# Bias lines made first and spread straight from SBUF, and one norm moved by a step, in a hybrid attention block

## The reference

```python
u = rmsnorm(h, attn_norm_g)
qa, ka, va, qb, kb, vb = split(u @ w_in)
oa = swa_sink_attention(qa, ka, va, sinks, rel_bias)   # 8 heads, chunks of 64, window of 128 keys, T5 bias
ob = diff_attention(qb, kb, vb, lam, ..., rel_bias)    # 4 heads, two softmaxes each, block-causal, T5 bias,
                                                       # then rmsnorm per head over its 128 columns
h = h + concat(oa, ob) @ w_out
h = h + square(relu(rmsnorm(h) @ w_up)) @ w_down
h = h + sigmoid(rmsnorm(h) @ w_gate) * (p @ w_ple)
y = rmsnorm(h, final_norm_g)
```

## Time and profile before

| | |
|---|---|
| median of 3 runs | 1303.7 us (1301.81 to 1304.3) |
| profiled execution | 1304.3 us, span 1302.5 us |
| TensorE busy (matmuls) | 1281.1 us, 98% of the span |
| VectorE, ScalarE, GpSimd busy | 445.5, 377.4, 478.9 us |
| mean granted TensorE clock | 0.993 of full speed |
| DMA | 82.91 MB, mean 64 GB/s |

### The profile page before, as it was taken

The page is one execution under the profiler, slowest core; times in us unless marked ns, Lnnn a source line. Parts: engine busy times, 40 slices in busy tenths (PEclk is TensorE's granted clock), DMA queues, the critical chain, the costliest instruction groups (busy, mean ns, idle before and its releaser), DMA issues.

```text
span 1302.5 us, 15895 instructions
## 1 busy us (share of the span) xinstructions
PE 1281.1 (98%) x6089; PEld 1026.7 (79%) x6089; DVE 445.5 (34%) x598; ACT 377.4 (29%) x690; POOL 478.9 (37%) x235
## 2 busy tenths in 40 slices
PE   7999999999999999999999999999999999999997
PEld 5777777777677888888888888888888888888886
DVE  5254655557765442211112211122111222223224
ACT  6344444455555422110011100111100112223221
POOL 3220202233335764322233322333222335675743
PEclk7999999999999999999999999999999999999999
DMA  6711101213512221111111111111111111113203
GB/s 225 259 33 33 33 17 33 49 50 97 146 34 78 84 81 38 47 49 46 49 47 50 47 48 48 48 48 48 48 48 48 48 48 49 48 58 92 61 1 130
DMA packets 139296, 82.91 MB, mean 64 GB/s; under 512 B 22185, under 2 KB 134870, under 8 KB 139126
## 3 DMA queue, kind: packets, MB, share of 16 engines
q1 hardware_dynamic: 138870, 81.19, 20.7%
q10 hardware_dynamic: 384, 1.15, 0.2%
HBM read 73.91 MB, written 10.77 MB: 65 GB/s over the span
## 4 chain that ended last, share of the span: by engine, by line
PE 94%; DVE 3%; ACT 1%; DMA 1%; issue 1%; SPq 0%; DVEq 0%; ACTq 0%
PE ps L994 61%; PE ps L1018 22%; PE ps L1127 3%; PE ps L1150 3%; PE ps L1138 1%; PE ps L1214 1%; PE ps L1200 1%; PE ps L1187 1%; DMA x_raw<-in_x 1%; ACT e_a L790 1%; PE ps L1060 1%; PE ps L1076 0%; PE ps L1031 0%; PE ps L1320 0%; DVE kmax L1559 0%
## 5 line engine op out<-in xcount | busy, mean ns | idle before, releaser
L527 POOL TENSOR_TENSOR w_lo<-w_raw,w_hi 128x1024 fp32r<-128x1024 f32 x110 | 268.7, 2443 | 723.9 <-ACT w_hi L698 453.6
L698 ACT CAST w_hi<-w_raw 128x1024 fp32r<-128x1024 f32 x70 | 73.9, 1055 | 452.3 <-PE ps L994 452.3
L994 PE MATMUL ps<-z_hi,w_hi 128*128 128x512 f32 x624 | 193.4, 391 | 0.0
L994 PE MATMUL ps<-z_lo,w_hi 128*128 128x512 f32 x624 | 192.2, 389 | 0.0
L994 PE MATMUL ps<-z_hi,w_lo 128*128 128x512 f32 x624 | 192.1, 389 | 0.0
L1018 PE MATMUL ps<-u_hi,w_hi 128*128 128x512 f32 x416 | 177.2, 426 | 1.7 <-DVE o_bt L1501 1.7
L1018 PE MATMUL ps<-u_hi,w_lo 128*128 128x512 f32 x416 | 164.3, 395 | 0.0
L1018 PE MATMUL ps<-u_lo,w_hi 128*128 128x512 f32 x416 | 163.8, 394 | 0.0
L994 PE MATMUL ps<-u_lo,w_hi 128*128 128x512 f32 x512 | 157.6, 389 | 0.0
L994 PE MATMUL ps<-u_hi,w_hi 128*128 128x512 f32 x512 | 157.6, 389 | 0.0
L994 PE MATMUL ps<-u_hi,w_lo 128*128 128x512 f32 x512 | 157.6, 389 | 0.0
(11 more groups left out here) (163 smaller groups left out, 1343.7 us busy)
## 6 DMA issues: line engine op xcount, KB each, us to landing
w_raw<-in_w_up SPq DMA_DIRECT2D x64, 256.0 KB, 3.0
w_raw<-in_w_down SPq DMA_DIRECT2D x64, 256.0 KB, 3.0
w_raw<-in_w_in SPq DMA_DIRECT2D x48, 256.0 KB, 3.3
x_raw<-in_x SPq DMA_DIRECT2D x8, 512.0 KB, 7.4
h_save<-x_t SPq DMA_DIRECT2D x1, 4096.0 KB, 12.4
h<-h_save SPq DMA_DIRECT2D x4, 1024.0 KB, 11.0
w_raw<-in_w_out SPq DMA_DIRECT2D x16, 256.0 KB, 2.8
w_raw<-in_w_out SPq DMA_DIRECT2D x32, 128.0 KB, 3.1
```

What stands on the lines that cost most here:

```text
L527: nc.gpsimd.tensor_tensor(w_lo[:, s * D:(s + 1) * D], w_raw[:, s * D:(s + 1) * D], w_hi[:, s * D:(s + 1) * D].bitcast(F32), ALU.subtract). ...
L698: nc.scalar.copy(w_hi[:, s * D:(s + 1) * D], w_raw[:, s * D:(s + 1) * D]).then_inc(hi_done, 1)
L994: mm = nc.tensor.matmul(o[i], w, xx[:, x0[i]], start=(first and n == 0), stop=(last and n == 2))
```

## The change

- TensorE makes the two line products before it turns the first tile of x, into banks 0 and 1; VectorE copies them to lines before its x loop; turn_x(2), whose target has the same banks, waits for the copies.
- line_once goes. save_lines writes rows straight from lines in SBUF, a source that repeats each line 128 times: those of B at the place of the old transfers, those of A behind h_save. SP waits for the first before the bands of B and for the second before those of A; VectorE's wait before soft_b is now for the second.
- root_b(3) on GpSimd moves from step 0 to step 1, behind split_lo(22); head_norm(3) on VectorE moves from the middle of step 2 to the end of step 1.

```diff
-        line_once = nc.dram_tensor("line_once", [12, LINE], F32).ap()
...
+            def save_lines(i0, i1, c0, saved):
+                rows = line_rows.rearrange("(i q l) -> i q l", q=P, l=LINE)
+                sp.dma_start(rows[i0:i1, :, :], lines[i0:i1, c0:c0 + LINE].unsqueeze(1).to_broadcast([i1 - i0, P, LINE])
+                             ).then_inc(saved, 16)
...
             sp.wait_ge(ln_sb, 2)
-            sp.dma_start(line_once[0:A_HEADS, :], lines[0:A_HEADS, 0:LINE]).then_inc(ln_out, 16)
-            sp.dma_start(line_once[A_HEADS:12, :], lines[A_HEADS:12, LINE:2 * LINE]).then_inc(ln_out, 16)
-            sp.wait_ge(ln_out, 32)
-            sp.dma_start(line_rows.rearrange("(i q l) -> i q l", q=P, l=LINE),
-                         line_once.unsqueeze(1).to_broadcast([12, P, LINE])).then_inc(ln_rows, 16)
+            save_lines(A_HEADS, 12, LINE, ln_out_b)
             load_q(0)
             load_v(1)
-            sp.wait_ge(ln_rows, 16)
+            sp.wait_ge(ln_out_b, 16)
             sp.wait_ge(lam_p, 1)
...
             sp.dma_start(h_save, x_t[:, :]).then_inc(h_saved, 16)
+            save_lines(0, A_HEADS, 0, ln_out_a)
             load_k(1)
             load_q(1)
+            sp.wait_ge(ln_out_a, 16)
...
GpSimd, step v of A (behind split_lo, ahead of head_lo):
-                if v == 0:
+                if v == 1:
                     root_b(3)
...
TensorE:
+            pe.wait_ge(hot_in, 32)
+            for i in range(2):
+                nc.tensor.matmul(ps[0:12, i * 512:i * 512 + LINE], relb[:, :], hot[:, i * LINE:(i + 1) * LINE],
+                                 start=True, stop=True).then_inc(ln_ps, 1)
+
             def turn_x(t):
                 pe.wait_ge(x_in[t], 16)
+                if t == 2:
+                    pe.wait_ge(ln_sb, 2)
...
-            pe.wait_ge(hot_in, 32)
-            for i in range(2):
-                pe.wait_ge(x_h, 3 + i)
-                nc.tensor.matmul(ps[0:12, (1 + 2 * i) * 512:(1 + 2 * i) * 512 + LINE], relb[:, :],
-                                 hot[:, i * LINE:(i + 1) * LINE], start=True, stop=True).then_inc(ln_ps, 1)
...
-            pe.wait_ge(ln_sb, 2)
             half_block(0, 1, range(DT)).then_inc(blk_done, 1)
...
VectorE:
+            for i in range(2):
+                dve.wait_ge(ln_ps, i + 1)
+                nc.vector.tensor_copy(lines[:, i * LINE:(i + 1) * LINE], ps[0:12, i * 512:i * 512 + LINE]
+                                      ).then_inc(ln_sb, 1)
             for t in range(TT + 1):
...
-                if t == 4:
-                    for i in range(2):
-                        dve.wait_ge(ln_ps, i + 1)
-                        nc.vector.tensor_copy(lines[:, i * LINE:(i + 1) * LINE],
-                                              ps[0:12, (1 + 2 * i) * 512:(1 + 2 * i) * 512 + LINE]).then_inc(ln_sb, 1)
...
-                if v == 2:
-                    head_norm(3)
...
                     sum_a(v + 2)
+                if v == 1:
+                    head_norm(3)
...
-            dve.wait_ge(ln_rows, 16)
+            dve.wait_ge(ln_out_a, 16)
```

More of the change, by code:

```diff
@@ L307, in build @@
         hot_in, ln_ps, ln_sb = sem("hot_in"), sem("ln_ps"), sem("ln_sb")
-        ln_out, ln_rows = sem("ln_out"), sem("ln_rows")
+        ln_out_b, ln_out_a = sem("ln_out_b"), sem("ln_out_a")
         lam_p, lam_e = sem("lam_p"), sem("lam_e")
```

## The result

The changed kernel takes 1337.9 us (median; 1337.0 to 1339.0) against 1303.7 us of the kernel before (1301.8 to 1304.3) on the same chip: ratio 1.0265, 95% interval 1.0247 to 1.0283. It is 2.65% slower, and the forecast was 1338. The profiled executions have spans of 1334.8 and 1302.5 us, so the trace has 32.3 us to explain.

The account below looks back on a forecast made before the run. The prediction took TensorE as the bound nearly everywhere. Its terms, 2.0 + 23.0 + 2.9 + 4.9 + 1.5 = 34.3 us over the profiled 1304.3 us, gave 1338.6 us, by the median 1338; range 1309 to 1350 us.

Parts of the forecast that it names:

- Line products: At the head of TensorE's queue: they delay the turn of x, so the dense matmuls begin 2.0 us later.
- two terms (2.0 + 23.0): Up to the first attention step: 2.0 us for the line products, 23.0 us of waiting for the rows' writes.
- Rows: Writes of B's and A's rows from SBUF: 30.0 us each, making the first attention step 23.0 us late.
- Clock behind the wait: After the first attention step's wait: TensorE's clock at half for 5.8 us, losing 2.9 us.
- Norm: Moved power and norm: score_a(5) comes 4.9 us later, and the clock falling in that gap costs 1.5 us.
- The engines' rate (1313): Rival for the rows' writes: 8.5 us each, hidden, leaving 8.4 us of loss; 1313 us, chance 0.27.
- The partition's share (1397): Rival for the rows' writes: 60 us each at a partition's proportional share; about 1397 us, chance 0.07.
- early clock: Rival at the start: full clock before the dense matmuls, saving 2.9 us and 0.7; 1300 us, chance 0.04.

Follow-up runs that it names:

- late_lines: The kernel before with the line products behind the turn of the last tile and the rows' transfers behind the first weight loads: 1304.7 us, ratio 1.0010.
- rows_only: The kernel before with only the rows written straight from SBUF, line products and norm as before: 1341.4 us, ratio 1.0292.
- lines_first: The kernel before with only the line products moved ahead of the turn of x: 1305.9 us, ratio 1.0019.
- spread: The changed kernel with its lines four partitions apart in SBUF: 1311.7 us, ratio 1.0063.
- spacing_two: The changed kernel with its lines two partitions apart in SBUF: 1311.2 us, ratio 1.0061.
- both_at_once: The changed kernel with A's write issued right behind B's, ahead of the weights: 1345.9 us, ratio 1.0331.
- rows_a_last: The changed kernel with A's write issued behind the loads of K1 and Q1: 1334.7 us, ratio 1.0246.

## Why the prediction was right

*Line products, 2.0 us.* Alone 2.3 us. The prediction took the half clock at the head for granted; the clock's column reads 1.00 there, in the changed kernel from 6 to 9 us, and yet the four passes took 2.66 us (6.07 to 8.73), as at 0.50 before, where late_lines has 1.38 us for them at 1.00. The duration carries the term, and not the column. In the change, 0.3 of the 2.3 us come from the load of the norm gains, which landed later in this execution (the transpose before them at 5.86 us; 5.57 in the trace before), and the chain was the one named: x_lo_v reached 2 at 23.7 us. But this delay does not reach the end by itself: the transpose at 99.25 us hangs on SP's list, and TensorE's wait before it is shorter by what it came later. As a sum of two terms (2.0 + 23.0) the step was right at 25.0 against 24.0; as two causes it was one, and early lines are a gain inside this change (rows_only). The clock rose at 29.6 us (0.70 over the window 29 to 30), 5.8 us after the dense start, as taken; lines_first and late_lines, with 2.9 and 3.1 us, show that this too could have come out otherwise.

*Rows, 30.0 us each.* B's write was issued at 14.37 us and waited for until 47.3; without issue (0.8) and the 2.4 us beside the moving that is 29.7 us. A's followed h_save (49.10 + 12.3 = 61.4) and its wait ended by 91.05: 29.6 us. That this value was met is in part luck. It was chosen between ends of 8.5 and 60 us on one weak pair of rows: a landing of 3.1 us, with the 2.4 us beside the moving that the prediction itself takes, says next to nothing of a rate. Nothing before the result showed why a sixteenth of 419 GB/s should be the step; spread and spacing_two now do. The forecast put the order right too: weight, split, mask, soft_b at 97.7 (96.64), e_small's transpose at 100.3 (99.25). Both came 1 us early: the second write ended by 91.05 us, forecast 93.1, and the weight behind it took 1.65 us until ScalarE's split, forecast 0.6. h_save and the write did not move side by side.

*A place that was passed over.* Q0's weight stands behind B's write as well. The prediction let SP wait there and asked only for what comes after; TensorE waited 0.5 us for it. It came out right by that margin, and two experiments, rows_only (14.1 us) and both_at_once (30.5 us), show what it would have cost.

*Clock behind the wait, 2.9 us.* 2.7. The engine stood idle for 20.8 us, the clock was at half and rose at 104.7 us (0.65 over the window 104 to 105), 5.4 us after the start.

*Norm, 4.9 and 1.5 us.* 4.7 and 0.8, together 5.5 for 6.4, and 5.7 alone. VectorE waited 3.88 us (3.9 forecast). The reading that head_norm would have to follow head_lo was right: it took 2.30 us from 352.60, of which 1.21 lie under head_lo. The clock term was too large in the time at half: the clock rose at 364.1 us, 4.3 us after score_a(5) began and not 5.8, which loses 2.1 us and not 2.9; the waits for the turned head, 1.7 us before and 0.6 now, took back 1.1 of it, close to the 1.3 that the prediction set off.

*The sum.* In the traces it is 2 us too high, 34.3 against 32.3 us: 1.0 in the first step, 0.2 each in its clock and in the norm's wait, 0.7 in the norm's clock. The medians lie 34.2 us apart, since the traced execution of before (1304.3 us) was the slowest of its kernel and that of after (1336.6 us) the fastest. That 1338 was met to 0.1 us is luck; that it was met within 2 or 3 us is not, but for the rate above.

*The rivals.* The prediction read the copy's 0.80 as twelve busy engines of sixteen; those are 0.75, and weights moved beside it. The engines' rate (1313) is excluded: the share agrees with four and eight engines, which is what the Trainium skill's rule ("DMA: Bandwidth & Descriptors", on why a DMA counts to 16) gives, but the rate does not follow the engines. That rival's time is, within 1.3 us, that of spread, where the source no longer limits. The partition's share (1397) is excluded by 200 GB/s out of eight partitions. No early clock came: it was at 0.50 from 20 to 29 us.

## What to carry to other kernels

Before a small tensor in SBUF is broadcast by DMA, count the groups of four partitions that it lies in, not its partitions: eight lines of 1.5 KB spaced four partitions apart were written at 200 GB/s, side by side at 53, and one copy by way of HBM cost nothing. What a slow transfer costs is found in the queue behind it: list all that SP issues later and when each is wanted, since the loads two places on (Q0, K1) decided here, and not who reads the rows; and ask when the source's own place is written again, for that was the wait left over in rows_a_last. An operation moved ahead on one engine must find its input ready in the other engine's list: here a power of 1.64 us behind a weight split cost some 3.7 us, and its reader's place ahead of the critical softmax 2 more.

## What the runs showed that was not expected

DMA engines count as busy while their source holds them back: 0.22 to 0.27 of sixteen at 25 and at 100 GB/s, and half of them at 53, 107 and 200 GB/s alike. And the hold-up between VectorE and GpSimd reaches whole instructions, in both directions: 3.41 us for a multiplication that takes 1.22, and then 2.27 us for GpSimd's 1.29.
